# Weight low parts of the mixer's first units after the context's norm, one unit converted inside a token norm, two tiles of the last output on GpSimd

## The chip, the cores and the metric

One core of a Trainium2 chip runs the whole layer in one launch. The metric is the device time of that launch in microseconds (us), lower is better. The engines are named as in the profile: PE is TensorE, DVE is VectorE, ACT is ScalarE, POOL is GpSimd, SP is SyncE, which here issues all transfers.

## The reference, cut to what matters

A macaron block on 1024 latent tokens and 256 context tokens, model width 1024, in float32:

```python
x   = x + 0.5 * m_x[2] * swiglu(modulate(rmsnorm(x, g0), m_x[0], m_x[1]), ffn1_w1, ffn1_w2)
ctx = ctx + 0.5 * m_c[2] * swiglu(modulate(rmsnorm(ctx, g0), ...), ffn1_w1, ffn1_w2)
px = modulate(rmsnorm(x, g1), m_x[3], m_x[4]) @ w_in
pc = modulate(rmsnorm(ctx, g1), m_c[3], m_c[4]) @ w_in
# retention over heads (latent scans start from the context's states), chunked gated MLP
x = x + m_x[5] * (concat(retention, gmlp) @ w_out)
x = x + 0.5 * m_x[8] * swiglu(modulate(rmsnorm(x, g2), m_x[6], m_x[7]), ffn2_w1, ffn2_w2)
return rmsnorm(x, final_g)
```

Three places of it matter here: the norms of the context and of the latent stream ahead of `w_in`, the first products with `w_in` (the context's keys and values), and the last norm with its output.

## The kernel before, in words

**Products.** A float32 product is made of three passes on PE with split operands: high times high, high times low, low times high. ACT makes the high part of a tile (a copy to fp32r), and DVE or POOL subtracts it from the tile to get the low part. Activations lie transposed, feature on the partition, in eight tiles of 128 features (`k` 0 to 7); the latent stream `X` has two halves of 512 tokens.

**Feed-forward.** Each of the two feed-forward parts ends in a down product (`down_product`, line 2209) of 77 steps in seven products of eleven. A step takes a pair of operands from a ring of six slots: SP loads it (line 647), ACT makes its high part (`ring_high`, line 1052), DVE its low part (`ring_low`, line 1623), and PE runs 12 matmuls on it (lines 2186 to 2188). DVE adds each finished product into `X` (`down_added`, line 1736). The last four steps of the last product are run tile by tile (`d` 0 to 3), so that the four tiles end one after another; `at_tile(d)` lets other work in behind each.

**Hooks.** Other work is written by hand between the steps: each engine's `mixer_opening(s)` runs behind its own handling of step `s`. During the first down product DVE also sums a piece of the modulation weights (`latent_sums`, lines 1443 and 1449).

**A norm** goes over five engines. ACT squares (line 935), DVE adds the squares (line 1313), PE sums over features with one-column matmuls (`norm_sum`, line 1996), DVE scales the mean (`norm_mean`, line 1323), POOL raises it to the power -0.5 (line 749), DVE spreads it onto diagonals (`norm_diagonal`, line 1326), PE broadcasts it into a PSUM bank (`norm_scale`, line 2006), DVE multiplies each tile with it (`scaled`, lines 1341 and 1753), ACT applies scale and shift (line 947) and makes the high part (line 942), POOL the low part (line 760). Each engine keeps its program order, so a waiting instruction holds all behind it.

**The context's norm** (place 1, block 0) is spread over the first down product: DVE's diagonal stands behind step 32, PE's `norm_scale` behind step 29, DVE's eight products (line 1753) behind step 34. PE waits for those before step 33, since that product writes the bank that held the scale. POOL, in its own order, does the context's rsqrt and then the low parts of the mixer's weight units 0 and 1 (`low(0)`, `low(1)`, line 743, 128x2048 each).

**The mixer's first fills.** The mixer is a list of bank fills. Fill 0 and 1 are the context's keys (units 0 and 1), 2 and 3 its values (units 2 and 3), fill 4 is the first of the latent stream (unit 4). Units use two slots in turn, so a unit's high part (`mix_high`, line 921) waits for the fill that used the slot before. Before fill 0, the latent norms of both token halves (place 1, blocks 1 and 2) are in flight. DVE makes the low parts of units 2, 3 and 4 (`unit_low`, line 1768) and evicts the keys (`context_keys`, line 1780).

**The tail.** The last norm sums its squares on PE (`square_sum`, line 2127, eight small matmuls each): behind tile `d` 2 it takes the first two sums of the second half, behind tile 3 the last three. Then comes the chain of the norm, `norm_out` on DVE (line 1347, eight tiles of 128x512, scaled by `final_g` and the PSUM scale), and SP's stores (line 728) of 256 to 1024 KB.

## Time and profile before

| what | value |
|---|---|
| median of 3 runs | 2052.42 us (2052.02 to 2053.18) |
| the profiled execution's own time | 2052.53 us |
| its span, first to last instruction | 2050.7 us |
| mean granted PE clock | 0.991 |
| busy: PE, DVE, ACT, POOL | 98%, 62%, 37%, 24% of the span |

The times of all rows are microseconds from the span's start. The profiled execution took 2052.53 us, 1.8 us more than its span and 0.1 us more than the median. A busy share near 100% says only that PE rarely waits; what a change may give or cost lies in the few places where PE does wait, or where its granted clock is 0.5, and in the end behind the last matmul.

### The profile page before, as it was taken

The numbers are of one execution on the slowest core, as the hardware profiler recorded it, in microseconds if no ns is written. First come the engines' busy times: TensorE is split into PE (matmuls) and PEld (weight loads), VectorE is DVE, ScalarE is ACT, GpSimd is POOL, SyncE is SP. The second block draws the span as 40 slices with busy tenths as digits, with TensorE's granted clock in tenths as the row PEclk, the third lists the DMA queues.
The fourth block names the chain that finished last, engine by engine and source line by source line (L and its number), as shares of the span: only waits on it lengthen the run. The fifth ranks groups of instructions, "written<-read, shape, count | busy, mean of one in ns | idle before, by whom it ended". The sixth has DMA issues, their size and how long they took to land.

```text
span 2050.7 us, 26021 instructions
## 1 busy us (share of the span) xinstructions
PE 2008.0 (98%) x10112; PEld 1689.4 (82%) x10112; DVE 1266.6 (62%) x1887; ACT 758.9 (37%) x1098; POOL 496.3 (24%) x311
## 2 busy tenths in 40 slices
PE   7999999999999998999999999999999999999997
PEld 5999988888888887888989898877788888888886
DVE  5988666556788678775454324468656555555555
ACT  4333533333333354445121221446333333334342
POOL 1000042333221103014222222554332421210001
PEclk9999999999999999999999999999999999999998
DMA  8964436666656786733101011121656644466664
GB/s 335 353 258 145 143 106 204 214 205 206 215 186 215 256 297 196 258 112 109 42 21 42 31 43 61 62 82 57 212 198 206 213 161 151 161 212 192 191 194 154
DMA packets 108762, 343.52 MB, mean 168 GB/s; under 512 B 11488, under 2 KB 20960, under 8 KB 90464
## 3 DMA queue, kind: packets, MB, share of 16 engines
q1 hardware_dynamic: 108640, 341.85, 49.1%
q8 instruction: 81, 1.33, 0.3%
q14 instruction: 41, 0.34, 0.1%
HBM read 267.36 MB, written 74.45 MB: 167 GB/s over the span
## 4 chain that ended last, share of the span: by engine, by line
PE 85%; issue 5%; DVE 5%; ACT 2%; DMA 1%; POOL 1%; DVEq 0%; POOLq 0%; SPq 0%; ACTq 0%
PE PS L2144 12%; PE PS L2146 12%; PE PS L2145 12%; PE PS L1986 8%; PE PS L1988 8%; PE PS L1987 8%; PE PS L2186 5%; PE PS L2188 5%; PE PS L2187 5%; PE PS L2102 4%; DVE WVL L1577 1%; PE PS L2362 1%; DMA WR<-w_units 1%; PE PS L2043 1%; PE PS L2023 0%
## 5 line engine op out<-in xcount | busy, mean ns | idle before, releaser
L2144 PE MATMUL PS<-HH,WVH 128*128 128x512 f32 x672 | 265.8, 395 | 0.0
L2146 PE MATMUL PS<-HH,WVL 128*128 128x512 f32 x672 | 263.7, 392 | 0.0
L2145 PE MATMUL PS<-HL,WVH 128*128 128x512 f32 x672 | 261.9, 390 | 0.0
L1986 PE MATMUL PS<-HH,WH 128*128 128x512 f32 x416 | 165.0, 397 | 2.9 <-DVE WL L1768 2.9
L1988 PE MATMUL PS<-HH,WL 128*128 128x512 f32 x416 | 162.0, 389 | 0.0
L1987 PE MATMUL PS<-HL,WH 128*128 128x512 f32 x416 | 161.9, 389 | 0.0
L1577 DVE TENSOR_TENSOR WVL<-WR,WVH 128x512 fp32r<-128x512 f32 x160 | 115.1, 720 | 72.3 <-ACT WVH L1004 72.3
L2146 PEld LDWEIGHTS PS<-HH,WVL 128*128 128x128 f32 x672 | 126.1, 188 | 29.9
L2145 PEld LDWEIGHTS PS<-HL,WVH 128*128 128x128 f32 x672 | 126.2, 188 | 27.8
L2144 PEld LDWEIGHTS PS<-HH,WVH 128*128 128x128 f32 x672 | 126.3, 188 | 26.5
L1623 DVE TENSOR_TENSOR DLOW<-DRAW,DHIGH 128x1024 fp32r<-128x1024 f32 x78 | 99.7, 1286 | 71.3 <-ACT DHIGH L1052 70.9
L1623 DVE TENSOR_TENSOR HL<-HLF,HH 128x1024 fp32r<-128x1024 f32 x76 | 102.7, 1361 | 61.1 <-ACT HH L1052 60.6
L1004 ACT ACTIVATE WVH<-WR 128x512 fp32r<-128x512 f32 x164 | 98.1, 623 | 96.2 <-PE PS L2146 80.3
L743 POOL TENSOR_TENSOR WL<-WR,WH 128x2048 fp32r<-128x2048 f32 x20 | 92.2, 4612 | 166.4 <-ACT WH L921 166.4
L1052 ACT ACTIVATE DHIGH<-DRAW 128x1024 fp32r<-128x1024 f32 x78 | 82.5, 1060 | 124.8 <-DMA DRAW<-down_weight_sums 73.8
L2186 PE MATMUL PS<-DHIGH 128*128 128x512 f32 x312 | 124.2, 398 | 0.0
L921 ACT ACTIVATE WH<-WR 128x2048 fp32r<-128x2048 f32 x47 | 89.6, 1906 | 90.0 <-PE PS L1988 90.0
L2187 PE MATMUL PS<-DLOW,DHIGH 128*128 128x512 f32 x312 | 122.7, 393 | 0.0
L2188 PE MATMUL PS<-DHIGH,DLOW 128*128 128x512 f32 x312 | 122.4, 392 | 0.0
L749 POOL TENSOR_TENSOR RS<-MS,NEGH 128x4 f32<-128x4 f32 (+3 forms) x16 | 22.9, 1434 | 404.9 <-DVE MS L1323 347.0
L1004 ACT ACTIVATE WVH<-ST 128x512 fp32r<-128x512 f32 x125 | 78.7, 631 | 111.1 <-PE PS L2146 66.1
L2186 PE MATMUL PS<-HH 128*128 128x512 f32 x304 | 119.4, 393 | 0.1
(282 smaller groups left out, 4974.5 us busy)
## 6 DMA issues: line engine op xcount, KB each, us to landing
WR<-w_units SPq DMA_DIRECT2D x89, 1024.0 KB, 5.8
gated<-HB SPq DMA_DIRECT2D x44, 512.0 KB, 6.6
down_weight_sums<-WB SPq DMA_DIRECT2D x22, 1024.0 KB, 3.8
gated_sums<-TBF SPq DMA_DIRECT2D x22, 768.0 KB, 4.1
AW<-ada_units SPq DMA_DIRECT2D x12, 1024.0 KB, 13.2
HLF<-down_weight_sums SPq DMA_DIRECT2D x46, 256.0 KB, 3.4
W2RB<-w_units SPq DMA_DIRECT2D x22, 512.0 KB, 3.6
WB<-w_units SPq DMA_DIRECT2D x22, 512.0 KB, 3.6
```

The costliest lines, as they stand in the source:

```text
L1004: act.activation(WVH[:, slot], src, ACT.Copy).then_inc(s_wh, 1)
L1577: dve.tensor_tensor(WVL[:, m], weight_block(m), WVH[:, m].bitcast(F32), ALU.subtract).then_inc(s_wl, 1)
L1623: dve.tensor_tensor(low_part, raw, high_part.bitcast(F32), ALU.subtract).then_inc(s_rl, 1)
L1986: pe.matmul(dst, wh, xh, start=first, stop=False)
L1987: pe.matmul(dst, wh, xl, start=False, stop=False)
L1988: return pe.matmul(dst, wl, xh, start=False, stop=last)
L2144: pe.matmul(bank[:, :], wh, xh, start=first, stop=False, skip_group_check=True)
L2145: pe.matmul(bank[:, :], wh, xl, start=False, stop=False, skip_group_check=True)
L2146: ins = pe.matmul(bank[:, :], wl, xh, start=False, stop=k == 3, skip_group_check=True)
L2186: pe.matmul(bank[:, :], wh, xh, start=j == 0 and i in (0, 1, 3), stop=False, skip_group_check=True)
L2187: pe.matmul(bank[:, :], wh, xl, start=False, stop=False, skip_group_check=True)
L2188: return pe.matmul(bank[:, :], wl, xh, start=False, stop=j == HALF - 1, skip_group_check=True)
```

## The change

It does four things. POOL's wait before `low(0)` and `low(1)` now holds them until PE has written the context's norm scale. The high part of unit 2 moves on ACT from behind the modulation of block 1 into it, before tile 5; on DVE the low part of unit 2 moves before the last added square of block 2, and the first key eviction before the norm's mean; on PE the sum and the scale of block 2's norm move one fill later. In the last norm, PE takes the square sum of tile 5 behind `d` 2, that of tile 6 before the last step of `d` 3, and only that of tile 7 at the end. For the output of the second half, ACT scales the tiles 0 and 1 by `final_g` in place and copies the PSUM scale into `RSB` in SBUF; POOL multiplies the two tiles with it; DVE waits for the copy and makes the other six; the store of tiles 0 and 1 comes second.

```diff
+        RSB = at("RSB", [P, TB], F32, W + 38912)
+        POOL_OUT = (0, 1)
...
-            stores = [(0, 0, 4), (0, 4, 8), (1, 0, 2), (1, 2, 4), (1, 4, 6), (1, 6, 7), (1, 7, 8)]
+            stores = [(0, 0, 4), (0, 4, 8), (1, 2, 4), (1, 0, 2), (1, 4, 6), (1, 6, 7), (1, 7, 8)]
             for b, k, end in stores:
-                sp.wait_ge(s_hf, 8 * J[3, b + 1] + end)
+                if (b, k) == (1, 0):
+                    sp.wait_ge(s_fgs, 2 * len(POOL_OUT) + 1)
+                else:
+                    sp.wait_ge(s_hf, 8 * J[3, b + 1] + end - (len(POOL_OUT) if b else 0))
...
             pool.wait_ge(s_col, ADA_STEPS[0])
+            pool.wait_ge(s_rb, J[1, 0] + 1)
             pool.wait_ge(s_tst, sums_stored(0, NF - 1))
             low(0)
             low(1)
...
             for b in (1, 2):
                 norm_rsqrt(3, b)
+            pool.wait_ge(s_fgs, len(POOL_OUT) + 1)
+            for k in POOL_OUT:
+                pool.tensor_tensor(OUT[1][:, k, :], X[:, k, TB:SEQ], RSB[:, :], ALU.mult).then_inc(s_fgs, 1)
...
                     square(1, 2, 4 + k // 2)
+                if k == 5:
+                    mix_high(2)
                 token_modulated(1, 1, k)
                 norm_high(1, 1, k, k + 1)
-            mix_high(2)
             mix_high(3)
...
             feed_forward(1, final_squares)
+            for k in POOL_OUT:
+                act.activation(X[:, k, TB:SEQ], X[:, k, TB:SEQ], ACT.Copy, scale=FG[:, k:k + 1]).then_inc(s_fgs, 1)
             for k in range(4):
                 final_square(12 + k, 1, 4 + k, 24 + k + 1)
+            act.wait_ge(s_rb, J[3, 2] + 1)
+            act.activation(RSB[:, :], scale_bank(3, 2)[:, :], ACT.Copy).then_inc(s_fgs, 1)
...
+            unit_low(2)
             add_square(1, 2, 7)
+            context_keys(0)
             norm_mean(1, 2)
-            context_keys(0)
             norm_diagonal(1, 2)
-            unit_low(2)
             context_keys(1)
             unit_low(3)
...
             norm_diagonal(3, 2)
-            norm_out(2, 0, KT)
+            dve.wait_ge(s_fgs, len(POOL_OUT) + 1)
+            norm_out(2, len(POOL_OUT), KT)
...
                             if d == 0:
                                 pe.wait_ge(s_rl, STEPS * f + s + 1)
+                            if d == 3 and s == STEPS - 1:
+                                at_tile(None)
                             ins = step_tile(s, d)
...
-                if n == 0:
+                if n == 1:
                     norm_sum(1, 2)
-                if n == 1:
+                if n == 2:
                     norm_scale(1, 2)
...
                 if d == 2:
                     pe.wait_ge(s_ms, J[3, 1] + 1)
-                    square_sum(1, 0, (s_qt[1], 3), first=True)
+                    square_sum(1, 0, (s_qt, 3), first=True)
                     square_sum(1, 4, (s_sqt, 13))
+                    square_sum(1, 5, (s_sqt, 14))
+                if d is None:
+                    square_sum(1, 6, (s_sqt, 15))
                 if d == 3:
-                    for k in range(5, KT):
-                        ins = square_sum(1, k, (s_sqt, 8 + k + 1))
-                    ins.then_inc(s_st, 1)
+                    square_sum(1, 7, (s_sqt, 16)).then_inc(s_st, 1)
```

The two semaphores `s_qt` are also joined into one that counts on; the work and the waits under them stay the same.

## Rows read from the trace of the kernel before

**Rows 1.** The page, part 1: busy time of the engines.

```profile
PE 2008.0 (98%) x10112; PEld 1689.4 (82%) x10112; DVE 1266.6 (62%) x1887; ACT 758.9 (37%) x1098; POOL 496.3 (24%) x311
```

**Rows 2.** Waits of TensorE, 740 to 960: us in total, times, longest.

```profile
PE PS L2006 <- DVE DG L1326: 5.7, 1, 5.7
PE PS L1986 <- DVE WL L1768: 2.7, 1, 2.7
PE PS L1996 <- DVE ACC L1313: 1.2, 1, 1.2
```

**Rows 3.** Timeline, 770 to 788: start, us, engine, line, tiles, count, [idle before].

```profile
770.14 1.71 POOL L749 TENSOR_TENSOR RS<-MS,NEGH 128x2 f32<-128x2 f32 x1 [74.24 <-DVE MS L1323]
771.82 9.19 POOL L743 TENSOR_TENSOR WL<-WR,WH 128x2048 fp32r<-128x2048 f32 x2
771.88 4.73 DVE L1326 TENSOR_TENSOR DG<-ID,RS 128x256 f32<-128x256 f32 x1 [0.60 <-POOL RS L749]
776.53 6.69 DVE L1623 TENSOR_TENSOR HL<-HLF,HH 128x1024 fp32r<-128x1024 f32 x2
776.66 1.22 PE L2006 MATMUL PS<-DG,ONES 128*128 128x256 f32 x2 [5.68 <-DVE DG L1326]
783.52 1.53 DVE L1449 SCALAR_TENSOR_TENSOR HHF<-HLF,CS,HHF 128x256 f32<-128x256 f32 x3
784.97 2.73 DVE L1753 TENSOR_TENSOR XC<-XC,PS 128x256 f32<-128x256 f32 x8
787.76 0.50 PE L2186 MATMUL PS<-HH 128*128 128x512 f32 x1
```

**Rows 4.** Timeline, 800 to 809: VectorE beside eight short GpSimd subtractions.

```profile
800.34 8.95 POOL L846 TENSOR_TENSOR HCL<-XC,HCH 128x256 fp32r<-128x256 f32 x8 [19.33 <-ACT HCH L1166]
806.08 2.61 DVE L1449 SCALAR_TENSOR_TENSOR HHF<-HLF,CS,HHF 128x256 f32<-128x256 f32 x3
```

**Rows 5.** Windows: stretch, length, busy of five engines (PE first), PEclk, DMA, GB/s.

```profile
774.20:781.10 6.90, 4.43 (x11) 3.49 (x12) 6.90 (x2) 1.06 (x1) 6.81 (x2) 0.51 0.02 4
902.40:907.40 5.00, 5.00 (x12) 3.94 (x13) 2.75 (x14) 0.00 (x0) 1.12 (x1) 0.50 0.00 0
924.40:927.90 3.50, 3.50 (x18) 3.50 (x18) 3.08 (x11) 2.09 (x2) 2.52 (x3) 0.51 0.82 290
943.90:946.50 2.60, 0.00 (x1) 0.00 (x0) 2.29 (x2) 1.61 (x3) 0.88 (x1) 1.00 0.00 0
2044.40:2050.00 5.60, 0.00 (x0) 0.00 (x0) 2.99 (x5) 0.00 (x0) 0.00 (x0) 0.50 0.99 372
```

**Rows 6.** Timeline, 913 to 947, the mixer's first fills.

```profile
913.60 2.68 POOL L760 TENSOR_TENSOR HL<-HF,HH 128x512 fp32r<-128x512 f32 x2 [8.89 <-ACT HH L942]
914.98 0.74 DVE L1736 SCALAR_TENSOR_TENSOR X<-PS,GATE,X 128x512 f32<-128x512 f32 x1
931.78 2.16 DVE L1780 TENSOR_SCALAR KC<-PS,Z 128x128 f32<-128x128 f32 x8 [1.83 <-PE PS L1988]
936.77 0.82 ACT L947 ACTIVATE HF<-HF,MODS,GAIN 128x512 f32<-128x512 f32 x1 [3.08 <-DVE HF L1341]
942.28 1.90 ACT L921 ACTIVATE WH<-WR 128x2048 fp32r<-128x2048 f32 x1
944.21 2.29 DVE L1768 TENSOR_TENSOR WL<-WR,WH 128x2048 fp32r<-128x2048 f32 x1 [3.87 <-ACT WH L921]
```

**Rows 7.** Timeline, 2034 to 2048, the last norm, the output and its first store.

```profile
2034.86 2.99 PE L2127 MATMUL PS<-ONES,HLF 128*128 128x1 f32 x24
2035.06 0.75 DVE L1736 SCALAR_TENSOR_TENSOR X<-PS,GATE,X 128x512 f32<-128x512 f32 x1 [0.64 <-PE PS L2188]
2035.85 0.63 ACT L1273 ACTIVATE HLF<-X 128x512 f32<-128x512 f32 x1 [2.73 <-DVE X L1736]
2042.03 5.36 DVE L1347 SCALAR_TENSOR_TENSOR OUT<-X,FG,PS 128x512 f32<-128x512 f32 x8 [2.17 <-PE PS L2006]
2043.46 0.37 SPq L728 DMA_DIRECT2D out<-OUT  x1
```

More of the change, by code:

```diff
@@ L376, in layer @@
         s_sqt = sem("final_squares_done")
-        s_qt = [sem(f"final_squares_added{t}") for t in range(2)]
+        s_qt = sem("final_squares_added")
         s_out = sem("stored")
+        s_fgs = sem("last_tiles_weighted_and_scaled")
         def release(n):
@@ L904, in _ @@
                 if n > 1:
-                    pool.wait_ge(s_qt[1], n - 1)
-                pool.tensor_tensor(SQT[1][:, 0, 0:TB], SQT[1][:, 0, 0:TB], SQT[1][:, n, 0:TB], ALU.add).then_inc(s_qt[1], 1)
+                    pool.wait_ge(s_qt, n - 1)
+                pool.tensor_tensor(SQT[1][:, 0, 0:TB], SQT[1][:, 0, 0:TB], SQT[1][:, n, 0:TB], ALU.add).then_inc(s_qt, 1)
             for n in range(1, KT):
@@ L909, in _ @@
                 if n > 1:
-                    pool.wait_ge(s_qt[0], n - 1)
+                    pool.wait_ge(s_qt, 3 + n - 1)
                 pool.tensor_tensor(SQT[0][:, 4, 0:TB], SQT[0][:, 4, 0:TB], SQT[0][:, (4 + n) % KT, 0:TB],
-                                   ALU.add).then_inc(s_qt[0], 1)
+                                   ALU.add).then_inc(s_qt, 1)
             for b in (1, 2):
                 norm_rsqrt(3, b)
+            pool.wait_ge(s_fgs, len(POOL_OUT) + 1)
+            for k in POOL_OUT:
+                pool.tensor_tensor(OUT[1][:, k, :], X[:, k, TB:SEQ], RSB[:, :], ALU.mult).then_inc(s_fgs, 1)
         @block.scalar
@@ L2412, in final_sum @@
                     pe.wait_ge(BS[1].fyd, 24)
-                    square_sum(0, 4, (s_qt[0], KT - 1), first=True).then_inc(s_st, 1)
+                    square_sum(0, 4, (s_qt, 3 + KT - 1), first=True).then_inc(s_st, 1)
             def final_norm(d):
```

## The prediction

> **What bounds the kernel now.** The page comes first: PE is busy 98% of the span [rows 1], so an edit pays only where PE waits, where its clock is low, or behind the last matmul. The waits of TensorE between 740 and 960 show three [rows 2]: 5.7 us for the diagonal of the context's norm, 1.2 us for the last added square of block 2, 2.7 us for a low part before fill 4. The timeline gives the reason of the first [rows 3]: DVE's diagonal, some 0.3 us of work, is recorded with 4.73 us, beside the first of POOL's two low parts (9.19 us for both). The two ring low parts behind it take 6.69 us instead of 2.4. DVE and POOL take turns there. The windows show where the clock is at its lower level, 1.2 GHz [rows 5]: after that wait, after a run of one-column matmuls, and after the 1.2 us wait. The last group is the tail [rows 7]: square sums, the norm's chain, eight output tiles, stores.
>
> **Edit 1, the low parts of units 0 and 1.** The rsqrt ends at 771.85 [rows 3]. With POOL free the diagonal is ready at 772.2, PE writes the scale from 772.3 instead of 776.66: 4.4 us earlier. PE then has that matmul pair and steps 30 to 32 before it. These took 776.66 to 787.65, of which 4.4 us were at half clock, so 8.8 us at full clock [rows 3, 5]. PE comes to step 33 at 781.1 instead of 787.65. This would be a gain of 6.6 us.
>
> But step 33 waits for DVE's eight products of the context, and before, these ended at 787.7 (784.97 plus 2.73), just as PE arrived (787.76) [rows 3]. So I have to follow DVE. After the diagonal it makes low part 33 until 773.4. POOL is released by the scale at about 773.0, so it stands first for the next turn: 773.4 to 778.0 (half of 9.19). Then low part 34, 1.15 us, to 779.1; then POOL's second, to 783.7; then the modulation sum (0.3 plus 1.53) to 785.5; then the eight products, 2.7 us, to 788.2. That they take turns one instruction each is read from two places: the diagonal slipped in between POOL's two instructions and the ring low part behind it waited for the second [rows 3]; and three modulation sums beside POOL's short subtractions took 2.61 us instead of 1.53 [rows 3, 4]. If low part 34 gets in before POOL, the sum is the same, since the modulation sum stands between it and the products. So the stall moves from the scale to step 33: PE waits 781.1 to 788.2, and is **0.4 us later** than before, not 6.6 earlier.
>
> The Trainium skill, SBUF — State Buffer, section "SBUF: two separate sides", says the pair of ports that VectorE and GpSimd share is an exclusive lock held for a whole instruction. That speaks against this edit, which moves 9.2 us of such instructions without shortening them; it doesn't say who gets the lock next.
>
> The clock: PE idles 7 us there. After the 5.68 us wait it came back at half clock and lost half of 4.43, 2.2 us; this lay before the join and cost nothing. After the new wait it is on the path. The three low stretches lost 2.2, 2.5 and 1.75 us [rows 5]; bounds 0 to 2.5, I take 1.5. Edit 1: **+1.9 us**. Units 0 and 1 are needed only after 916, so their own lateness costs nothing; the context's low parts on POOL follow at 800 as before.
>
> **Edit 2, unit 2 inside the norm.** What it removes: PE's 1.2 us before the norm's sum, and the half clock of 924.4 to 927.9 [rows 2, 5]. Fill 1 then ends near 927.7 instead of 931.75. What it adds: ACT, at tile 5 by 920, waits for fill 0 to end (922.2), then converts 1.9 us, so it takes up tile 5 at 924.1. Its period is 1.38 us a tile (936.77 to 942.28 for four [rows 6]), with one square among them (0.6): tile 7's high part comes at 928.8, its low part on POOL at 930.8, as POOL takes turns with DVE's low part of unit 2 and the last added square. POOL's rsqrt stands behind it in order: 931.8, diagonal 932.5, then the second key eviction 2.0 and the low part of unit 3, 2.3 [rows 6]: 936.7, where the first product of block 2 can begin. Before, the same place was 936.1 (931.78 plus 2.0 plus 2.3). The chain from there to fill 4 is copied unchanged: four tiles and the conversion on ACT, the low part on DVE (944.21 plus 2.3), fill 4 at 946.6 [rows 2, 6]. So fill 4 comes **0.6 us later**, though fills 1 to 3 are earlier: what they win is spent waiting before fill 4. That wait grows from 2.65 to about 5 us. At 2.65 us the clock stayed up (1.00 in the window before it); at 5.68 us it fell [rows 5]. Bounds 0 to 2.5; 5 is nearer 5.68, so I take 1.5. Edit 2: **+2.1 us**. SP's table loads wait for the added squares and come 5 us later, on a queue that is idle then.
>
> **Edit 3, the square sums.** A sum costs about 0.9 us of PE (2.99 for three [rows 7]). Before, all three stood behind the last step, where two of them ran beside what the third needs anyway: DVE's addition (0.75) and ACT's square (0.63), 2035.02 to 2036.5, with PE reaching the third sum at 2036.56. Now two stand ahead of the last step, so tile 7's matmuls end 1.8 us later (2036.8), the square at 2038.25, the third sum at 2039.3 instead of 2037.85: **+1.45 us**. The operands of the two moved sums are ready; their waits cost nothing.
>
> **Edit 4, two tiles on POOL.** DVE now starts after ACT's copy of the scale, which the trace does not show; an ACT instruction of 128x512 is 0.63 [rows 7]. DVE's eight tiles take 5.36, six take 4.0. That is 0.7 us less on DVE. POOL's two take 2.7 [rows 6], from the same moment, so they are done first. ACT's two scalings lie in the 2 us and more that it idles earlier: nothing. But the last window says what ends the kernel: 372 GB/s from 2044.4 to 2050.0 [rows 5], the 2.1 MB of the second half without a gap, though the first store is issued 1.4 us after DVE's start [rows 7] and the last at 2047.4. The end hangs on the first store. It still needs two DVE tiles, and DVE starts 0.65 later: **+0.65 us**. Store two needs POOL's tiles at 3.3 us, when the first is still under way.
>
> **Sum.** 1.9 + 2.1 + 1.45 + 0.65 = 6.1 us. The low-clock stretch 902.4 to 907.4 cost 2.5 us, one of the dearest places a fall can take; with the work shifted it may lose less, 0 to 1.5 back, I take 0.7. So +5.4: the profiled execution's 2052.53 becomes 2057.9; against the median, 2057.8. A measurement here tells 0.2%, 4.1 us, from no change.
>
> **Rivals.**
> - *DVE keeps its turn* (0.15). If DVE holds its place through its back-to-back instructions, the modulation sums and the eight products end before 781 and PE never waits at step 33. The place is step 33, the point from which it decides is products done by 781.1. The 6.6 us are then gained; with no fall of the clock before fill 4 the rest is 0.6 + 1.45 + 0.65 - 0.7 = +2.0: 2047.8, faster. With a fall there, 2049.3. Against it speak the two places named above.
> - *No clock falls on the path* (0.13): the waits move as I say, but PE resumes at full clock: 0.4 + 0.6 + 1.45 + 0.65 = +3.1, 2055.5.
> - *The output is bound by DVE, not by the stores* (0.05): edit 4 gives 0.7 instead of costing 0.65: 2056.5. The full transfer window speaks against it.
> - *POOL and DVE block each other in the output* (0.05). The first store would wait for two DVE tiles with a POOL tile between, 1.3 us: 2059.1. Against it: an addition from PSUM and one SBUF tile took 0.74 beside POOL's subtractions, and 0.75 without [rows 6, 7]. The Trainium skill, same page and section, lets a VectorE instruction contend if it has two SBUF inputs; if the column of `final_g` counts as one, this rival is what the rule gives.
>
> **Numbers.** My forecast has 0.62, with its own range 2054 to 2060.5 (the clock terms from 0 to 2.5 each). The whole range reaches to the first rival's dearer form: 2049.5 to 2060.5. Slower by over 0.2% is above 2056.5: four fifths of the forecast and the last rival, 0.56. Faster is half of the first rival and what I may have missed, 0.12. The rest is 0.32.
>
> **What would show it.** Right: the diagonal of the context's norm under 1 us; a new wait of TensorE of about 7 us before step 33, ended by the XC products; one of about 5 us before fill 4; the wait before the norm's sum down to under 1 us; the last square sum at 2039 plus what the rest adds, alone; stores again at some 370 GB/s without a gap. Wrong: no wait at step 33, fill 4 reached by a wait as short as before, or a gap between the stores.

## The result and the profile after

The changed kernel takes 2063.43 us (median of 5 runs, 2057.71 to 2066.32). The kernel before, run beside it, takes 2053.07 us (5 runs, 2052.02 to 2053.19). The ratio is 1.0049 [1.0032, 1.0065]: 10 us slower. That is the side I forecast, but twice the size, and above my range.

The changed kernel's profiled execution took 2066.32 us, with a span of 2064.5 us, so it is the longest of the five. The page's part 1, and from its part 5 the group with the new wait:

```profile
PE 2015.8 (98%) x10112; PEld 1693.8 (82%) x10112; DVE 1266.2 (61%) x1885; ACT 761.2 (37%) x1101; POOL 500.2 (24%) x313
...
L2202 PE MATMUL PS<-HH 128*128 128x512 f32 x304 | 120.6, 397 | 6.6 <-DVE XC L1768 6.6
```

The same 10112 matmuls keep PE busy 7.8 us longer than in [rows 1]. The number of matmuls is unchanged, so over half of the 13.8 us between the two spans is busy time, which the windows below put down to a lower clock, and not waiting. The idle before L2202, the first matmul of a step, is all one wait.

The waits of TensorE between 740 and 965, to set beside [rows 2]:

```profile
PE PS L2202 <- DVE XC L1768: 6.6, 1, 6.6
PE PS L2002 <- DVE WL L1783: 5.1, 2, 4.4
PE PS L2022 <- DVE DG L1341: 1.6, 1, 1.6
PE PS L2012 <- DVE ACC L1328: 0.6, 1, 0.6
```

The waits have moved, not gone. The diagonal's wait fell from 5.7 to 1.6 us and the one for the added square from 1.2 to 0.6. In their place stand 6.6 us before step 33, ended by the eight products XC, and 4.4 us before fill 4, ended by a low part of the mixer. In all 13.9 us instead of 9.6.

The timeline of the context's norm (start, duration, count, and in brackets the idle before), to set beside [rows 3]:

```profile
771.15 1.71 POOL L755 TENSOR_TENSOR RS<-MS,NEGH 128x2 f32<-128x2 f32 x1 [74.42 <-DVE MS L1338]
774.30 10.13 POOL L749 TENSOR_TENSOR WL<-WR,WH 128x2048 fp32r<-128x2048 f32 x2 [1.44 <-issue]
772.89 0.42 DVE L1341 TENSOR_TENSOR DG<-ID,RS 128x256 f32<-128x256 f32 x1 [0.60 <-POOL RS L755]
773.24 6.78 DVE L1638 TENSOR_TENSOR HL<-HLF,HH 128x1024 fp32r<-128x1024 f32 x2
779.94 4.64 DVE L1458 TENSOR_SCALAR HHF<-HLF,CS 128x256 f32<-128x256 f32 x1
784.61 1.52 DVE L1464 SCALAR_TENSOR_TENSOR HHF<-HLF,CS,HHF 128x256 f32<-128x256 f32 x3
786.05 2.73 DVE L1768 TENSOR_TENSOR XC<-XC,PS 128x256 f32<-128x256 f32 x8
```

The diagonal now takes 0.42 us. POOL's first low part starts at 774.30 and DVE's second ring low part waits it out; POOL's second catches the first modulation sum (L1458, 4.64 us). The products end at 788.8, in this execution 1.1 us later than before. PE itself is 1.1 us later at step 33, 0.7 to 1.0 of it from the first 45 us of the kernel on, so relative to PE they come when they came before.

Windows (stretch, length, busy time of PE, PEld, DVE, ACT and POOL, granted clock, DMA share, GB/s), to set beside [rows 5]:

```profile
786.20:793.00 6.80, 4.16 (x10) 3.33 (x11) 6.80 (x14) 4.96 (x8) 0.00 (x0) 0.50 0.43 147
902.30:912.50 10.20, 10.20 (x35) 8.90 (x35) 3.31 (x15) 0.00 (x0) 1.12 (x1) 0.50 0.00 0
922.70:929.00 6.30, 6.30 (x58) 6.30 (x57) 3.37 (x5) 4.09 (x6) 2.71 (x3) 1.00 0.59 217
950.10:956.80 6.70, 5.22 (x12) 4.13 (x13) 3.21 (x4) 5.02 (x8) 4.96 (x4) 0.50 0.47 157
1458.60:1462.00 3.40, 3.40 (x9) 2.69 (x9) 1.70 (x3) 0.39 (x1) 0.00 (x0) 0.50 0.55 205
2042.30:2045.70 3.40, 3.40 (x9) 2.66 (x10) 1.36 (x3) 0.06 (x1) 0.00 (x0) 0.50 0.86 321
2058.10:2063.80 5.70, 0.00 (x0) 0.00 (x0) 1.75 (x3) 0.00 (x0) 0.25 (x1) 0.50 0.98 368
```

About half of the busy PE time of a window at 0.50 is lost. So 2.1 us are lost behind the wait of step 33, 2.6 behind the wait of fill 4, 1.7 at 1458, and 1.7 on the last tile: four places that ran at full clock before, or whose loss lay before a join. The fall at 902, which was there before, lasts 10.2 us. Before, it reached by the granted clock from 900.5 to 907.4, 6.8 us, of which [rows 5] shows the last 5.0. The one at 924 is gone (1.00). The last window is the stores of block 2: 368 GB/s without a gap, as in [rows 5].

The tail, to set beside [rows 7]:

```profile
2039.56 2.73 PE L2143 MATMUL PS<-ONES,HLF 128*128 128x1 f32 x24
2045.88 0.95 PE L2143 MATMUL PS<-ONES,HLF 128*128 128x1 f32 x8
2047.66 0.75 DVE L1751 SCALAR_TENSOR_TENSOR X<-PS,GATE,X 128x512 f32<-128x512 f32 x1 [4.00 <-PE PS L2204]
2048.45 0.63 ACT L1284 ACTIVATE HLF<-X 128x512 f32<-128x512 f32 x1 [6.09 <-DVE X L1751]
2049.13 1.87 PE L2143 MATMUL PS<-ONES,HLF 128*128 128x1 f32 x8 [1.50 <-ACT HLF L1284]
2055.18 0.60 ACT L1301 ACTIVATE RSB<-PS 128x512 f32<-128x512 f32 x1 [6.10 <-PE PS L2022]
2055.81 4.04 DVE L1362 SCALAR_TENSOR_TENSOR OUT<-X,FG,PS 128x512 f32<-128x512 f32 x6 [2.80 <-ACT RSB L1301]
2055.85 2.50 POOL L924 TENSOR_TENSOR OUT<-X,RSB 128x512 f32<-128x512 f32 x2 [3.57 <-ACT RSB L1301]
```

The three sums of the tiles 0, 4 and 5 now stand in a row ahead of the last tile (2.73 us of one-column matmuls), that of tile 6 stands inside it, and that of tile 7 stands alone (1.87 us).

**Where the 13.8 us between the two profiled spans arise**, by how much later the same matmul starts than before: 0.7 us by the 11th microsecond and 1.0 by the 45th; 1.1 at step 33; 3.0 behind the half clock there; 4.65 behind the stretch at 902; 5.0 at fill 4 (951.58 instead of 946.56); 7.5 behind its half clock; 9.2 behind the one at 1458, and still 9.25 where the last run of sums begins (2039.56 instead of 2030.31 us); 13.15 at the end of the last sum (2051.00 instead of 2037.85); 13.8 at the end. The first 1.0 us is before anything the change touches: there the clock rose later (at 11.4 us instead of 9.7), and I count it to the execution, not to the change. In the 18 profiled executions of this document PE is between 0.3 us earlier and 2.1 us later at 700 us than in that of the kernel before.

Two more shares belong in part or whole to the execution, as two kernels were profiled twice. The stretch at 902 lasts 6.8 us in one profiled execution of edit 2 alone and 3.4 in the other, and the same holds for edit 3 alone. The fall at 1458 stands in one of the two executions of edit 2 and in one of the two of edit 3, and in 9 of all 18. So of the 13.8 us some 4.4 (1.0, 1.65 and 1.7) can't be put down to the change by one trace.

### The profile page after: what moved, and what is told of

Read it like the earlier page. It is cut to its first block, busy times and chain, and to the rows that moved or that the text cites. A ratio compares the mean times of both kernels' runs of the same rounds, so it can differ in the third digit from the quotient of the medians.

```text
span 2064.5 us, 26025 instructions
## 1 busy us (share of the span) xinstructions
PE 2015.8 (98%) x10112; PEld 1693.8 (82%) x10112; DVE 1266.2 (61%) x1885; ACT 761.2 (37%) x1101; POOL 500.2 (24%) x313
## 4 chain that ended last, share of the span: by engine, by line
PE 55%; DVE 4%; ACT 2%; POOL 1%; issue 1%; DMA 0%; DVEq 0%; ACTq 0%; POOLq 0%
PE PS L2160 6%; PE PS L2162 6%; PE PS L2161 6%; PE PS L2002 6%; PE PS L2004 6%; PE PS L2003 6%; PE PS L2202 5%; PE PS L2203 5%; PE PS L2204 5%; PE PS L2380 1%; DVE WVL L1592 1%; PE PS L2400 0%; DVE KZ L1904 0%; PE PS L2361 0%; DVE WL L1783 0%
## 5 line engine op out<-in xcount | busy, mean ns | idle before, releaser
L2202 PE MATMUL PS<-HH 128*128 128x512 f32 x304 | 120.6, 397 | 6.6 <-DVE XC L1768 6.6
L2202 PE MATMUL PS<-DHIGH 128*128 128x512 f32 x312 | 123.9, 397 | 0.0
L2204 PE MATMUL PS<-HH,HL 128*128 128x512 f32 x304 | 120.0, 395 | 0.0
```

The source lines that it names most:

```text
L2202: pe.matmul(bank[:, :], wh, xh, start=j == 0 and i in (0, 1, 3), stop=False, skip_group_check=True)
L2204: return pe.matmul(bank[:, :], wl, xh, start=False, stop=j == HALF - 1, skip_group_check=True)
```

## The experiments

Each is an edit of the kernel before, so a gain or loss is against that kernel, and its lines are numbered a little differently from both others. "Before" below means the kernel before as run on the same chip beside it.

**Part 1: each edit alone.**

*Edit 1 alone*, on POOL ahead of `low(0)` and `low(1)`.

```
+            pool.wait_ge(s_rb, J[1, 0] + 1)
```

> Edit 1 alone: GpSimd's low parts of units 0 and 1 wait for the context's norm scale. My theory (the two engines take turns, so the stall only moves): TensorE's wait for the diagonal shrinks to 1 to 2 us, a wait of 6 to 7 us ended by the XC products stands before step 33, step 33 starts within 0.6 us of its time before, and the half clock after that wait costs 1.5 to 2.5 us, with a later fall that may come out longer: median 2 to 4 us over before. Rival (VectorE keeps its turn): no wait at step 33, 5 us or more under before. Rival (the clock is innocent): within 1 us of before.

Measured: 2055.24 us (11 runs) against 2052.28, ratio 1.0016 [1.0008, 1.0025], some 3.3 us. Of its four waits of TensorE in the same stretch, the two longest:

```profile
PE PS L2187 <- DVE XC L1754: 6.6, 1, 6.6
PE PS L1987 <- DVE WL L1769: 2.7, 1, 2.7
```

The 6.6 us before step 33 belong to edit 1, and fill 4's wait without edit 2 stays at 2.7 us.

*Edit 2 alone*, run twice: ACT converts unit 2 ahead of tile 5 of the norm, DVE makes its low part ahead of the last added square, PE sums and scales one fill later.

```
+                if k == 5:
+                    mix_high(2)
-            mix_high(2)
...
+            unit_low(2)
...
+            context_keys(0)
             norm_mean(1, 2)
-            context_keys(0)
...
-            unit_low(2)
...
-                if n == 0:
+                if n == 1:
                     norm_sum(1, 2)
-                if n == 1:
+                if n == 2:
                     norm_scale(1, 2)
```

> Edit 2 alone: the conversion of unit 2 inside the token norm with the orders that go with it on VectorE and TensorE. My theory: the wait before the norm's sum falls under 1 us and fills 1 to 3 come earlier, but fill 4 starts 0 to 0.8 us later behind a wait of 4 to 5 us, and the clock falls there: 2 to 3 us over before. Rival (fill 4's time is set elsewhere, the wait costs only its own length): 0 to 1 us over before. Rival (the edit works as meant): 1 us or more under before.

> Edit 2 alone again, on the same chip and beside the same runs of the kernel before as its version with extra matmuls, as their comparison: 2 to 4 us over before, wait before fill 4 of 4.4 us, clock at its lower level behind it.

Measured: 2056.11 against 2052.28, ratio 1.0015 [1.0006, 1.0024]; again, 2054.74 against 2052.80, ratio 1.0013 [1.0004, 1.0022]. Both show the 4.4 us wait. The window just behind fill 4's start in the first:

```profile
945.00:951.00 6.00, 4.13 (x10) 3.27 (x11) 3.60 (x4) 4.31 (x7) 3.94 (x3) 0.50 0.51 175
```

The 4.13 us that PE was busy there ran at half clock. The fall behind fill 4 comes with edit 2, and the one ahead of fill 1 goes: it is in none of the four profiled executions with edit 2 in them (wait of 0.6 us before the norm's sum), and in 10 of the 13 whose wait there is 1.2 us.

*Edit 3 alone*, run twice. All three square sums but the last are moved ahead of the last tile or the last step, as in the change.

```
+                            if d == 3 and s == STEPS - 1:
+                                at_tile(None)
...
+                    square_sum(1, 5, (s_sqt, 14))
+                if d is None:
+                    square_sum(1, 6, (s_sqt, 15))
-                    for k in range(5, KT):
-                        ins = square_sum(1, k, (s_sqt, 8 + k + 1))
-                    ins.then_inc(s_st, 1)
+                    square_sum(1, 7, (s_sqt, 16)).then_inc(s_st, 1)
```

> Edit 3 alone: the square sums of tiles 5 and 6 ahead of the last step. My theory: the norm's mean comes 1.45 us later by the two sums alone, and up to 2 us more in executions where the clock falls on the last tile because three sums in a row stand before it: 1.4 to 3.5 us over before, with a wide spread. Rival (the sums were what held the mean, so it comes earlier): 0.5 us or more under before.

> Edit 3 alone again, beside the same runs of before as the kernel with full matmuls in the same place, as their comparison: 4.5 to 7 us over before.

Measured: 2057.75 (6 runs) against 2052.28, ratio 1.0030 [1.0018, 1.0041]; again, 2055.91 (9 runs) against 2051.88, ratio 1.0021 [1.0012, 1.0031]. That is 6.2 and 4.3 us for an edit that I had put at 1.45, and neither interval takes that in (0.07%). The first is also far above what I expected before this run (1.4 to 3.5), the second just under what I expected of the repeat. The last tile of the second, timeline of PE:

```profile
2029.91 2.73 PE L2127 MATMUL PS<-ONES,HLF 128*128 128x1 f32 x24
2032.50 0.78 PE L2186 MATMUL PS<-DHIGH 128*128 128x512 f32 x1
...
2039.49 1.87 PE L2127 MATMUL PS<-ONES,HLF 128*128 128x1 f32 x8 [1.50 <-ACT HLF L1273]
```

and its windows before and behind the end of the sums:

```profile
2029.50:2032.50 3.00, 3.00 (x27) 2.92 (x26) 3.00 (x5) 1.00 (x2) 0.00 (x0) 1.00 0.27 104
2032.50:2035.90 3.40, 3.40 (x10) 2.72 (x10) 1.52 (x3) 0.21 (x1) 0.00 (x0) 0.50 0.86 322
```

PE is busy all through the sums, yet the clock is 0.50 from the matmul behind them: 3.40 us of the last tile at half clock, 1.7 lost, as in the changed kernel. In the first run's trace it fell later and stayed down longer. The sums end at 2034.6, three full matmuls of the last tile still ran at 1.00, and from 2035.4 the clock was 0.50 up to the end:

```profile
2031.50:2035.40 3.90, 3.90 (x31) 3.69 (x30) 3.90 (x7) 1.24 (x2) 0.00 (x0) 1.00 0.44 165
2035.50:2037.70 2.20, 2.20 (x6) 1.69 (x6) 0.55 (x1) 0.00 (x0) 0.00 (x0) 0.50 0.77 287
```

There the stretch from the start of the sums to the end of the last one grew by 4.9 us, in the second run by 3.9. All three profiled executions with the whole of edit 3 have a fall on the last tile, and none of the other fifteen has.

*Edit 4 alone*: the change's own lines for `RSB`, `POOL_OUT`, the stores and the semaphores, of which these are the core.

```
+            pool.wait_ge(s_fgs, len(POOL_OUT) + 1)
+            for k in POOL_OUT:
+                pool.tensor_tensor(OUT[1][:, k, :], X[:, k, TB:SEQ], RSB[:, :], ALU.mult).then_inc(s_fgs, 1)
...
+            act.activation(RSB[:, :], scale_bank(3, 2)[:, :], ACT.Copy).then_inc(s_fgs, 1)
...
+            norm_out(2, len(POOL_OUT), KT)
```

> Edit 4 alone: two output tiles on GpSimd, VectorE behind ScalarE's copy of the scale. My theory (the stores' transfer ends the kernel and starts 0.65 us later): 0.6 to 0.7 us over before from the scale's matmul to the end, VectorE's six tiles 4.0 us, the transfer again 5.6 us without a gap. Rival (VectorE bounds the output): 0.7 us under before. Rival (the engines block each other): 1.3 us or more over before, VectorE's tiles at over 0.8 us each.

Measured: 2052.82 (11 runs) against 2052.28, ratio 1.0003 [0.9994, 1.0012]: 0.6 us, at the lower edge of the forecast and not told apart from nothing. Its trace has the copy at 0.60 us and DVE's six tiles at 4.04, as in the changed kernel.

The four add up to 11 to 13 us (3.3 + 2.7 to 3.1 + 4.3 to 6.2 + 0.6), the whole change to 10 (6.6 to 13.3 by its interval). The intervals are wide, so this shows only that no large term comes from their combination.

**Part 2: who gets its turn at the context's norm.** My account says that POOL and DVE take turns instruction by instruction. If so, short POOL instructions should hurt DVE little, wherever they start, and long ones nothing once they start behind the products.

*Low parts in pieces*, without any wait added:

```
+                if count <= FIRST_UNITS + 2:
+                    for k in range(KT):
+                        ins = pool.tensor_tensor(WL[:, slot, k], WR[:, slot, k], WH[:, slot, k].bitcast(F32), ALU.subtract)
...
```

> The kernel before with one change: GpSimd's low parts of units 0 and 1 in eight pieces of 128x256 each, with no wait added. My theory (one instruction each in turn): every VectorE instruction with two SBUF inputs there waits at most one piece, 0.6 to 0.7 us, so the diagonal is recorded with 0.8 to 1.1 us, TensorE waits 1.5 to 2.5 us for it, and the XC products end near 783 to 784, which leaves 2 to 3 us of wait at step 33: 3 to 5 us under before. Rival (the port stays with GpSimd over its back-to-back instructions): the diagonal again 4 us or more, no gain.

Measured: 2047.59 (11 runs) against 2052.77, ratio 0.9977 [0.9968, 0.9986]. Its timeline:

```profile
771.54 0.95 DVE L1331 TENSOR_TENSOR DG<-ID,RS 128x256 f32<-128x256 f32 x1 [0.60 <-POOL RS L754]
772.41 3.43 DVE L1628 TENSOR_TENSOR HL<-HLF,HH 128x1024 fp32r<-128x1024 f32 x2
776.62 2.60 DVE L1454 SCALAR_TENSOR_TENSOR HHF<-HLF,CS,HHF 128x256 f32<-128x256 f32 x3
779.15 2.72 DVE L1758 TENSOR_TENSOR XC<-XC,PS 128x256 f32<-128x256 f32 x8
...
771.48 15.90 POOL L745 TENSOR_TENSOR WL<-WR,WH 128x256 fp32r<-128x256 f32 x16
```

The DVE instructions with two operands in SBUF are now longer by about one short piece each and not by one long one: the diagonal 0.95 us instead of 4.73 [rows 3], the two ring low parts 3.43 instead of 6.69. So what a DVE instruction loses goes by the length of the POOL instruction beside it, as with turns, and not as if the two shared SBUF at a fixed rate. POOL pays with 15.90 us instead of 9.19, which nobody waits for. The products, which read one operand from PSUM, take 2.72 us, the same with and without POOL. They end at 781.9 instead of 787.7. Two things differ from what I expected: the products end 1 to 2 us earlier, and in this execution the clock fell again behind the 2.6 us wait before fill 4 (0.50 from 938.5 to 941.9), where it had stayed up in the kernel before.

*The wait, put one place later*: behind the products and not behind the scale.

```
+            pool.wait_ge(s_xm, 8 * (J[1, 0] + 1))
```

> The kernel before with GpSimd's low parts of units 0 and 1 held until VectorE has written the context's eight products. My theory (it is the order against the products that counts): no wait of over 0.5 us at step 33, TensorE there at 781 to 782 instead of 787.8, and the 9 us of contention falls on ring low parts, which have some steps of slack but not much: 3 to 6.5 us under before, less if TensorE comes to wait for a ring low part. Rival (the contention costs the same wherever it lies): within 1 us of before.

Measured: 2045.58 (6 runs) against 2052.77, ratio 0.9969 [0.9957, 0.9980]. Waits of TensorE, 740 to 965, all of them:

```profile
PE PS L1987 <- DVE WL L1769: 2.6, 1, 2.6
PE PS L2007 <- DVE DG L1327: 1.4, 1, 1.4
PE PS L1997 <- DVE ACC L1314: 1.2, 1, 1.2
```

No wait before step 33 is left. The same idea as edit 1, with another semaphore, turns a loss of 3.3 us into a gain of 6.4. The only difference in the code is whether POOL's two low parts (9 to 11 us) lie in front of the products or behind them. In the trace the clock stays at 1.00 there, since the long wait is gone.

*The wait of edit 1, filled.* If the wait costs by itself, matmuls in it change nothing; if it costs by the clock, they win. It is edit 1 and, before step 33, matmuls that write a bank whose content nothing uses.

```
+                            pe.wait_ge(s_hi, FIRST_UNITS + 2)
+                            pe.wait_ge(s_fyd, 6)
+                            for _ in range(26):
+                                pe.matmul(PS[1][:, :], WH[:, 1, 0, 0:P], WH[:, 0, 0:2, :], start=True, stop=True,
+                                          skip_group_check=True)
```

> Edit 1 alone, and 26 extra matmuls of 128x512 on TensorE before its wait at step 33, into a bank that the next product clears; their results are used by nothing. They take 5.9 us of the 6.6 us wait. My theory (the clock fell because TensorE had nothing to run, and that is what the moved wait costs): the granted clock stays 1.00 through step 33, step 33 starts at the same time as with edit 1 alone, and the kernel is 1.5 to 2.5 us faster than with edit 1 alone. Rival (the clock does not depend on that wait): same time as edit 1 alone.

Measured: 2051.97 (11 runs) against 2052.77, ratio 0.9995 [0.9986, 1.0004]. Its window and that of edit 1 alone, in this order:

```profile
788.00:792.00 4.00, 3.60 (x16) 2.99 (x17) 4.00 (x7) 3.09 (x6) 0.00 (x0) 1.00 0.35 122
```

```profile
788.00:792.50 4.50, 3.59 (x9) 2.82 (x10) 4.50 (x8) 3.58 (x6) 0.00 (x0) 0.50 0.20 70
```

With idle PE in front the next 3.6 us of matmuls run at 0.50, with busy PE in front at 1.00. By the ratios this gives 4.3 us back, and by the medians, each to its own before, 3.8; that is more than the 1.5 to 2.5 I expected, and the window of the changed kernel showed only 2.1. Where the rest comes from is open. Within the intervals the whole loss of edit 1 is the clock. Twenty-six matmuls whose results nothing uses make the kernel with edit 1 faster.

**Part 3: the wait before fill 4.**

*The same filling on top of edit 2*, with matmuls of `HH` on itself into a bank that nothing reads.

```
+                if n == 4:
+                    pe.wait_ge(s_hl, 8 * (J[1, 1] + 1))
+                    for _ in range(17):
+                        pe.matmul(PS[5][:, :], HH[:, 0, 0:P], HH[:, 0, 0:TB], start=True, stop=True,
+                                  skip_group_check=True)
```

> Edit 2 alone, and 17 extra matmuls of 128x512 on TensorE before its wait ahead of fill 4, into the bank of fill 5; their results are used by nothing. They take 3.9 us of the 4.4 us wait. My theory (a longer wait there is what brings the clock down): the granted clock stays 1.00 between 940 and 960, fill 4 starts at the same time as with edit 2 alone, and the kernel is 1.5 to 3 us faster than edit 2 alone, run here again. Rival (the clock falls by where it stands in time, whatever TensorE does): same as edit 2 alone.

Measured: 2052.66 (11 runs), against 2052.80 for before and 2054.74 for edit 2 on the same chip; ratio to before 1.0000 [0.9992, 1.0009]. The windows behind fill 4, first this kernel, then edit 2 alone, whose fall reaches from 946.4 to 949.8 and so takes in half of the window:

```profile
948.00:952.00 4.00, 4.00 (x19) 3.31 (x18) 0.27 (x1) 3.94 (x6) 3.18 (x3) 1.00 0.56 227
```

```profile
948.00:952.00 4.00, 4.00 (x15) 3.20 (x14) 0.00 (x0) 3.94 (x5) 3.83 (x3) 0.77 0.46 195
```

So edit 2 also costs through the clock: 2.1 us by the medians, and the 11 runs of this kernel end at 2054.47 where those of edit 2 alone reach from 2053.34 to 2058.91. Without the fall it comes out at nothing, though the wait before the norm's sum is halved and the half clock ahead of fill 1 is gone.

*Only the norm's sum one fill later*, ACT left as it was:

```
+            context_keys(0)
             norm_mean(1, 2)
-            context_keys(0)
...
-                if n == 0:
+                if n == 1:
                     norm_sum(1, 2)
-                if n == 1:
+                if n == 2:
                     norm_scale(1, 2)
```

> Edit 2 without its ScalarE part: the norm's sum and scale one fill later on TensorE, the first key eviction before the mean on VectorE, the conversion of unit 2 where it was. My theory: TensorE's 1.2 us wait goes, fill 1 runs at full clock and ends near 928; the diagonal no longer waits for a late tile 7, and the second key eviction and the low part of unit 3 come earlier, so fill 4 starts 1 to 3 us earlier with no longer a wait than before: 1 to 3 us under before. Rival (fill 1's end does not set fill 4): within 0.5 us of before.

Measured: 2060.61 (5 runs) against 2052.77, ratio 1.0039 [1.0026, 1.0053]. This was a miss. Its longest wait of TensorE and the DVE rows behind it:

```profile
PE PS L1986 <- DVE WL L1768: 9.1, 2, 4.9
```

```profile
929.20 0.69 DVE L1326 TENSOR_TENSOR DG<-ID,RS 128x512 f32<-128x512 f32 x1 [1.12 <-POOL RS L749]
929.81 2.28 DVE L1768 TENSOR_TENSOR WL<-WR,WH 128x2048 fp32r<-128x2048 f32 x1
```

I had left the low part of unit 2 behind the diagonal on DVE. With the sum one fill later the diagonal comes later, fill 2 stands behind it, and PE waits twice. Behind both waits the clock fell too (0.50 from 930.0 to 936.8 and from 950.4 to 957.3). It shows why the change had to move unit 2 and the norm together, and isn't a smaller version of it.

*The products before the low part of unit 3*, on top of the later wait (`s_xm`):

```
-            unit_low(3)
...
+                if k == 4:
+                    unit_low(3)
```

> The kernel before with GpSimd's low parts of units 0 and 1 held until the context's eight products are done, and VectorE's first four products of block 2's norm ahead of the low part of unit 3 instead of behind it. My theory (the chain to fill 4 runs from those products over ScalarE): fill 3 waits up to 1 us more for its low part, fill 4 starts about 2 us earlier than with the first edit alone, its wait falls from 2.6 to under 1 us: 5 to 9 us under before, 1 to 2.5 under the same kernel without the second edit. Rival (what fill 3 loses, fill 4 doesn't win back): no faster than without it.

Measured: 2045.46 (5 runs) against 2052.80, ratio 0.9960 [0.9948, 0.9973]; the wait before fill 4 goes from 2.6 to 1.4 us, not under 1 as I expected. Against the kernel with the later wait alone this isn't told apart: the two intervals overlap.

**Part 4: the sums of one column.**

*One sum moved instead of two*:

```
+                    square_sum(1, 5, (s_sqt, 14))
-                    for k in range(5, KT):
+                    for k in range(6, KT):
```

> Half of edit 3: the square sum of tile 5 behind d 2, those of tiles 6 and 7 at the end as before. My theory: one sum of 0.9 us ahead of the last tile moves its addition 0.9 us later, while one sum less stands before tile 7's; the mean comes 0.8 to 0.9 us later at full clock, and three sums in a row before the last tile can bring the clock down on it for up to 2 us more: 0.8 to 3 us over before. Rival (the sums at the end are what holds the mean): 0.5 us or more under before.

Measured: 2054.73 (11 runs, 2051.86 to 2057.66) against 2052.80, ratio 1.0007 [0.9998, 1.0015]. Inconclusive: it lies between nothing and edit 3. Its trace, of the fastest of the eleven, says one thing: the same run of three sums, 24 matmuls in 2.73 us, stands before the last tile, and the clock stayed at 1.00 through it and the whole tile. So such a run doesn't bring the clock down in every execution.

*The same delay, with full matmuls*: the sums stay where they were, and eight 512-column matmuls stand before the last step. That is the place of edit 3's one sum inside the tile, not of the third in the run ahead of it.

```
+                            if f and d == 3 and s == STEPS - 1:
+                                _, _, hp = SLOTS[s % NSLOT]
+                                for _ in range(8):
+                                    pe.matmul(PS[1][:, :], hp[:, 1, 0:P], hp[:, 0, :], start=True, stop=True,
+                                              skip_group_check=True)
```

> The kernel before, with eight extra matmuls of 128x512 (1.8 us at full clock) ahead of the last step of the second down product, where edit 3 puts square sums of about the same length; their results are used by nothing, and the sums stay where they were. If edit 3 costs 6 us because thin one-column matmuls there let the clock fall on the last tile, this kernel, with the same delay in full matmuls, costs only the delay: 1.3 to 2.5 us over before, 3 us or more under edit 3. If it is a delay of the last tile that costs 6 us, whatever runs in it, it costs the same as edit 3.

Measured: 2053.78 (11 runs) against 2051.88, ratio 1.0013 [1.0004, 1.0022], with edit 3 on the same chip at 1.0021 [1.0012, 1.0031]. The clock over the last tile:

```profile
2035.00:2041.00 6.00, 6.00 (x39) 5.30 (x37) 2.29 (x4) 0.86 (x2) 0.00 (x0) 1.00 0.80 298
```

The full matmuls cost about their own time (1.9 us by the medians, 2.7 by the ratio) and the clock stays up. By the ratios the two kernels aren't told apart; 2.1 us lie between their medians, where I expected 3 or more. The granted clock of the same tile is 1.00 here and 0.50 in edit 3. So a delay of the last tile by 1.8 us costs its own time and isn't what brings the clock down. What does, this kernel doesn't show: in edit 3 the clock fell before PE reached the place of these matmuls, and here only two sums stand ahead of the tile.

*The column sums at 900, spread*. In the kernel before they follow the eight matmuls of the norm's sum without a break:

```profile
897.85 4.52 PE L2033 MATMUL PS<-ONES,HHF 128*128 128x1 f32 x32
```

Now three of the eight latent columns stand one step and three two steps earlier, the other two in their old place.

```
+                if s in (STEPS - MAJOR - 3, STEPS - MAJOR - 2):
+                    pe.wait_ge(BS[0].fyd, 24)
+                    j = 3 * (s - STEPS + MAJOR + 3)
+                    for a in ADA_STEPS[j:j + 3]:
+                        latent_columns(a)
...
-                    pe.wait_ge(BS[0].fyd, 24)
...
-                    for a in ADA_STEPS:
+                    for a in ADA_STEPS[6:]:
```

> The kernel before, with the 32 one-column matmuls that sum the last modulation units (with the eight of the norm's sum they make one run of 5.3 us) spread behind three steps of the first down product, 12, 12 and 8. Work and count are the same. My theory (one long thin run brings the clock down): no stretch of lower clock near 900, 2 to 3.5 us under before. Rival (the thin matmuls cost only their own time): within 0.5 us of before.

Measured: 2050.82 (11 runs) against 2051.88, ratio 0.9996 [0.9988, 1.0005]. Its window where the clock fell before:

```profile
900.00:904.00 4.00, 4.00 (x27) 3.56 (x26) 1.92 (x13) 0.00 (x0) 0.91 (x1) 1.00 0.00 0
```

No half clock is left there, and PE is 2.85 us ahead at 907 in the two profiled executions. The two kernels with the sums spread, this and the next, have no fall at that place, and all sixteen other profiled executions have one. This shows that the run of 40 one-column matmuls brings the clock down. But the times show only 0.8 to 1.1 us, not the 2 to 3.5 I expected, and the interval takes in zero. The fall can be taken away; what it is worth in the mean of many runs stays unresolved.

**A version that beats both**: the later wait, the products first, the columns spread.

> The low parts after the context's products, the first four products of block 2 ahead of the low part of unit 3, and the one-column sums spread, all on the kernel before. If the gains add, as they lie in different places: 7.3 us of the first two and 2 to 3.5 us of the third, 9 to 11 us under before. If the clock gives back what one of them wins: 6 to 8 us.

Measured: 2043.76 us (5 runs, 2042.11 to 2043.97) against 2051.88, ratio 0.9962 [0.9949, 0.9976], 8 us faster than before and, by the two ratios, some 18 faster than the change. That is less than the 9 to 11 us I gave it if the gains add, and at the upper end of what I gave it if the clock gives something back. The kernel with the first two edits alone has the ratio 0.9960, so the third adds nothing that the times show. All waits of TensorE that are left between 740 and 965:

```profile
PE PS L1988 <- DVE WL L1769: 1.4, 1, 1.4
PE PS L2008 <- DVE DG L1327: 1.3, 1, 1.3
PE PS L1998 <- DVE ACC L1314: 1.2, 1, 1.2
```

Its windows show 1.00 for all of 774 to 793, 900 to 912, 924 to 936 and 945 to 957. The fall behind the 1.2 us wait and the norm's sum is still there, only earlier: the clock is 0.50 from 915.7 to 919.1.

## Why the prediction was right and where it failed

Every place that I had named as a test came out as named, but for the last square sum, which was 2.45 us later than 2039.3 plus the 9.25 us that the rest had added by then. The mechanism held for the waits and for the output. It lacked a fall of the clock on the last tile, and the sum failed.

- **Edit 1, the wait.** Forecast: the diagonal under 1 us, PE waiting 7.1 us before step 33, that step 0.4 us later. Measured: 0.42 us, 6.6 us, 0.0 once the 1.1 us that PE was late already are taken off. The rival "DVE keeps its turn" (0.15) falls: its products would have ended by 781.1 and they ended at 788.8. The turns are shown by the pieces and by the later wait. The Trainium skill, SBUF — State Buffer, section "SBUF: two separate sides", says that the shared pair of ports is locked for a whole instruction; the 4.64 us of the first modulation sum beside a POOL low part agree.
- **Edit 1, the clock.** Forecast 1.5 us, measured 2.1 in the window, and 3.8 to 4.3 by filling the wait. I had taken a value in the middle of my bounds of 0 to 2.5, though the fall behind the 5.68 us wait of before had cost 2.2 [rows 5] and the new wait was longer. The near row should have been taken whole; even that is 2.2, and why filling the wait gave back more is open.
- **Edit 2.** Forecast: fill 4 0.6 us later behind a wait of 5 us, and 1.5 for the clock. Measured: 0.4 us later, a 4.4 us wait, 2.5 us for the clock. In total 2.7 to 3.1 alone against 2.1: the same error as in edit 1, half as large.
- **Edit 3: this is the step that failed most**, "+1.45 us". Alone it measured 4.3 and 6.2; in the changed kernel's trace the stretch from the start of the sums to the end of the last one grew by 3.9 (7.54 to 11.44 us), and in the two of edit 3 alone by 4.9 and 3.9. Its working counted PE time only. The last tile's addition came 3.35 us later and not 1.8, because nine matmuls of the last tile ran at half clock. And the last sum took 1.87 us, at half clock after its wait, where I had given it 1.05 (2038.25 to 2039.3). 1.45 + 1.55 + 0.8 = 3.8. That the clock fell there is measured in all three traces with edit 3; that the three sums in a row bring it down is likely, by the run at 900, but not shown: the kernel with one sum moved has the same run and no fall in its one trace. I had written, of [rows 5], that the clock was low "after a run of one-column matmuls", and then didn't apply it to an edit that makes the run before the last tile from two sums into three.
- **Edit 4.** Forecast +0.65, measured 0.65 in the trace and 0.6 alone. All its steps came in: the copy 0.60 us (0.63), six tiles 4.04 (4.0), POOL's two 2.50 (2.7) beside them without blocking, stores without a gap. Both rivals on the output fall by the traces, as the times can't tell 0.6 us: POOL's tiles and DVE's six run in the same 4 us, each at its own speed, and the stores set the end.
- **The stretch at 902, -0.7 us.** It had the wrong sign in the profiled execution: 1.65 us were lost, since the low clock lasted to 912.5. It is a fall that exists in both kernels, and its length changes between executions of one kernel (6.8 and 3.4 us, for edit 2 and for edit 3). Its price was too low as well: with the sums spread PE comes out 3.1 us earlier and not 2.5.
- **A term that wasn't there**: the clock fell again at 1458.6, +1.7 us. It stands in 9 of 18 profiled executions, not in that of the kernel before, and in one of two each of edit 2 and edit 3. So the kernel alone doesn't decide it; what does is open.

"No clock falls on the path" (0.13) falls too. With what the changed kernel's trace shows for each term, the sum is 0.0 + 1.9 for edit 1, 0.4 + 2.5 for edit 2, 3.9 for edit 3 and 0.65 for edit 4: 9.35 us instead of 6.1. Of the 3.25 us between them 2.45 are edit 3's. The medians differ by 10.4 and the ratio gives 10.1, with an interval of 6.6 to 13.3, so the 9.35 fits, and how much the stretches at 902 and 1458 add in the mean isn't shown. That the direction came out right isn't luck, since each of the four edits cost about what it was forecast to cost, or more.

Open: how much of edit 3 (4.3 to 6.2 by the times, 3.9 and 4.9 in the traces) goes beyond its own delay and the clock; what brings the clock down on its last tile; and why the stretch at 902 lasts 3.4, 6.8 or 10.2 us and that at 1458 comes in some executions and not in others.

## What to carry to other kernels

When PE is at 98%, a long wait can cost its length and then the half clock behind it, so write both into the sum, and take the price of the clock from the nearest row whole. In these stretches the clock fell behind every wait of 4.4 us or more, and behind those of 2.6 or 2.7 us before fill 4 in one execution of eleven. When an edit moves matmuls of one column, look at what stands on both sides of them: a run of them is busy time, and the clock can still fall. When POOL and DVE fight over SBUF, don't ask only whether a long POOL instruction can start later, but which DVE chain it will stand in front of then, and hold it until that chain is through, or cut it into pieces.

## What was unexpected of the hardware

- Twenty-six matmuls with no use, put into a wait, made the kernel with edit 1 3.8 to 4.3 us faster, and seventeen before fill 4 that with edit 2 some 2.1 to 2.7. Neither is faster than the kernel before by its interval.
- A run of 40 one-column matmuls kept PE busy all through, and the clock fell in it or within 1 us behind it in 16 of 16 profiled executions; with the run cut into 12, 12 and 16 it fell in none of two. A run of 24 (2.73 us) before the last tile was followed by the lower clock within 1 us in three executions and not in a fourth. With 16 of them in the same place before, in 1.84 us, it stayed at 1.00. The Trainium skill, TensorE: Matmul & The Clock Gate, section "HAM oscillation — how this bites in real kernels", names gaps in which PE is idle as what brings the clock down. Here the clock fell in and behind a busy stretch of narrow matmuls.
- A `TENSOR_SCALAR` of 128x256 with one large operand in SBUF was held as long as one with two (4.64 us beside a POOL low part, 0.34 without POOL), and the 128x512 operation with one SBUF tile, one PSUM tile and a column wasn't held at all (4.04 us for six, beside POOL).
- Sixteen pieces of 128x256 cost POOL 15.90 us where two of 128x2048 cost 9.19, both beside a busy DVE.
